# Eight more tokens a layer by gathered expert rows: 152 dense columns, a ring of twelve tiles, the picks turned at tile 60

## The reference, cut to what matters

```python
def peer_ffn(h, w_q, sub_keys, u_tab, v_tab):
    ...
        v_half, i_half = lax.top_k(sc, PEER_TOPK_HALF)
        ...
        top_s, pos = lax.top_k(cand, PEER_TOPK)
        expert = jnp.take_along_axis(cand_idx, pos, axis=-1)
        g = jax.nn.softmax(top_s, axis=-1)
        u = u_tab[expert]
        act = jax.nn.gelu(jnp.einsum('thkd,td->thk', u, xc).astype(jnp.float32), approximate=False)
        w = (g * act).astype(xc.dtype)
        return jnp.einsum('thk,thkd->td', w, v_tab[expert])
```

## Time and profile before

| | us |
|---|---|
| median of 3 runs | 1905.86 |
| lowest, highest | 1900.08, 1906.43 |
| profiled execution, device time | 1903.83 |
| its span, first to last instruction | 1902.1 |
| TensorE busy | 1857.0 |
| VectorE busy | 1354.1 |
| ScalarE busy | 484.7 |
| GpSimd busy | 442.0 |

### The profile page before, as it was taken

The page is one execution under the profiler, slowest core; times in us unless marked ns, Lnnn a source line. Parts: engine busy times, 40 slices in busy tenths (PEclk is TensorE's granted clock), DMA queues, the critical chain, the costliest instruction groups (busy, mean ns, idle before and its releaser), DMA issues. The chain is left out here.

```text
span 1902.1 us, 35435 instructions
## 1 busy us (share of the span) xinstructions
PE 1857.0 (98%) x13794; PEld 1768.2 (93%) x13794; DVE 1354.1 (71%) x2860; ACT 484.7 (25%) x898; POOL 442.0 (23%) x412
## 2 busy tenths in 40 slices
PE   8999999999999999999999999999999999999998
PEld 7888887878999899999999998899989999999998
DVE  6899886795799767677754347769996776776442
ACT  6557644565411100000000046552110000000001
POOL 0000000000046343333343200002454333334330
PEclk9999999999999999999999999999999999999999
DMA  6554325533979999999999953287999999999995
GB/s 249 215 205 181 122 83 169 175 100 124 341 246 407 409 408 409 406 405 401 401 401 410 383 188 122 86 295 273 336 409 408 409 404 396 408 399 396 409 410 200
DMA packets 148012, 580.26 MB, mean 305 GB/s; under 512 B 13596, under 2 KB 13724, under 8 KB 145216
## 3 DMA queue, kind: packets, MB, share of 16 engines
q1 hardware_dynamic: 91712, 376.37, 51.9%
q0 software_dynamic: 56192, 202.47, 27.4%
HBM read 576.62 MB, written 1.05 MB: 304 GB/s over the span
## 5 line engine op out<-in xcount | busy, mean ns | idle before, releaser
L2682 PE MATMUL bank<-e_hidden,wbuf 128*128 (+1 forms) x4096 | 566.9, 300 | 0.0
L2682 PEld LDWEIGHTS bank<-e_hidden,wbuf 128*128 128x128 f32 x4096 | 557.7, 190 | 0.0
L2631 PE MATMUL bank<-h_dense,wbuf 128*128 128x160 f32 x3712 | 520.8, 301 | 8.3 <-DMA wbuf<-in_peer_u 6.8
L2631 PEld LDWEIGHTS bank<-h_dense,wbuf 128*128 128x128 f32 x3712 | 506.2, 190 | 14.1 <-issue 7.7
L276 ACT ACTIVATE tile_hi<-wbuf 128x1024 fp32r<-128x1024 f32 (+2 forms) x117 | 121.9, 1047 | 376.6 <-PE bank L2682 286.7
L284 DVE TENSOR_TENSOR tile_lo<-wbuf,tile_hi 128x1024 fp32r<-128x1024 f32 (+2 forms) x117 | 140.1, 1210 | 87.5 <-ACT tile_hi L276 86.8
L2471 POOL DMA_INDIRECT e_gbuf<-in_peer_rows,e_row_at x128 | 131.7, 1029 | 300.3 <-PE bank L2631 219.4
L2471 POOL DMA_INDIRECT e_gbuf<-in_peer_v,e_row_at x128 | 142.1, 1111 | 236.7 <-PE bank L2682 157.1
L2771 ACT ACTIVATE e_hidden<-bank 128x320 f32<-128x320 f32 x128 | 55.9, 437 | 518.7 <-PE bank L2631 518.6
L2492 DVE SCALAR_TENSOR_TENSOR x_tok<-e_gbuf,e_acts,x_tok 128x1024 f32<-128x1024 f32 x128 | 164.0, 1281 | 32.2 <-DMA e_gbuf<-in_peer_v,e_row_at 24.9
L386 PE MATMUL bank<-a_parts,tile_hi 128*128 128x512 f32 x512 | 178.2, 392 | 0.0
(11 more groups left out here) (408 smaller groups left out, 2651.4 us busy)
## 6 DMA issues: line engine op xcount, KB each, us to landing
wbuf<-in_peer_v SPq DMA_DIRECT2D x128, 1024.0 KB, 9.8
wbuf<-in_peer_u SPq DMA_DIRECT2D x116, 1024.0 KB, 11.8
wbuf<-in_w_in SPq DMA_DIRECT2D x16, 2048.0 KB, 7.4
wbuf<-in_peer_q SPq DMA_DIRECT2D x32, 512.0 KB, 4.5
wbuf<-in_hyb_in SPq DMA_DIRECT2D x16, 512.0 KB, 3.8
e_gbuf<-in_peer_u SPq DMA_DIRECT2D x8, 1024.0 KB, 10.7
wbuf<-in_mla_uq SPq DMA_DIRECT2D x9, 512.0 KB, 3.4
wbuf<-in_mla_in SPq DMA_DIRECT2D x8, 528.0 KB, 5.3
```

Source lines behind the costliest of these rows:

```text
L2631: last = nc.tensor.matmul(bank[:, j // 2 % 2, j % 2 * S:j % 2 * S + DENSE], tile[:, k * P:(k + 1) * P], h_dense[:, k, :], start=(k == 0), ...
L2682: last = nc.tensor.matmul(turned_x(g, k)[:, 0:DENSE], deep[:, slot, k * P:(k + 1) * P], hidden[:, bass.ds(a, 1), 0:DENSE].rearrange("p a t ...
```

## The change

Eight more tokens (`RARES`) of the dense ones go by rows: 152 columns are left. Each shares the partitions of a block in sixteen parts of eight picks, so they take 8 gathers of U and 8 of V, at the end of each list: 208 gathers a layer, paced as before between tiles 8 and 240. Their row numbers, shares and copies of x come by 48 small DMAs (three for each group of eight partitions), which POOL issues ahead of gathers 56 to 71. They count in `moved`, and ScalarE's wait behind pair 38 is now for all of them (`ALL_MOVED`), as is the one ahead of the tile that overwrites their source. Their sum has a buffer of its own (`sum_rare`), set to zero by VectorE, and a third matmul for each k in the fold.

The ring has twelve tiles (`DEEP`), over all three weight buffers, and four tiles are loaded early, not sixteen. U then starts at another place of the ring, so V does too (`V_PAIR`). The next layer's weights are loaded at slightly other points, and VectorE's first three roundings for them wait until the V tiles in their place are used. The picks are turned behind tile 60, not 56. A group more of eight dense tokens is gone, 19 a half.

```diff
 GATHERED = 64
 FEWS = 32
-DENSE = S - GATHERED - FEWS
+RARES = 8
+DENSE = S - GATHERED - FEWS - RARES
 HIDDEN = DENSE
-EARLY_TILES = 16
+SLOTS = 4
+EARLY_TILES = 4
+DEEP = 3 * SLOTS
...
-            "deep": wbuf[:, 0:2, :].rearrange("p w (j c) -> p (w j) c", c=TILE),
+            "deep": wbuf[:, 0:3, :].rearrange("p w (j c) -> p (w j) c", c=TILE),
...
-    FEW = slice(DENSE - P, GATHERED)
+    FEW, RARE = slice(GATHERED - FEWS, GATHERED), slice(GATHERED - FEWS - RARES, GATHERED - FEWS)
     SHARED = PICKS // 2
     EARLY = 2 * GBUFS
-    DOTS = SHARED + FEWS
+    DOTS = SHARED + FEWS + RARES
     ITEMS = 2 * DOTS
     FEW_BLOCK = [(slice(FEWS * n, FEWS * n + FEWS), slice(FEWS * n, FEWS * n + FEWS)) for n in range(P // FEWS)]
+    RARE_BLOCK = [(slice(RARES * n, RARES * n + RARES), slice(RARES * n, RARES * n + RARES)) for n in range(P // RARES)]
     MOVED = DMA * len(FEW_BLOCK)
+    ALL_MOVED = 3 * MOVED + 3 * DMA * len(RARE_BLOCK)
...
-    early = ([gbuf[:, 2 * n:2 * n + 2, :] for n in range(GBUFS // 2)] + [whole_tiles(56), whole_tiles(24)]
-             + [g["wbuf"][:, 2, :].rearrange("p (j c) -> p j c", c=TILE)[:, 2 * n:2 * n + 2, 0:D] for n in range(2)])
+    early = [gbuf[:, 2 * n:2 * n + 2, :] for n in range(EARLY_TILES // 2)]
...
+    x_rare = sb(f"{tag}_x_rare", [P, D])
+    sum_rare = stage[:, 76 * S:80 * S]
...
-    LAST_ROUND = NKEYS - STEP
-    EARLY_ROUNDS = EARLY_TILES // STEP
+    PAIRS, STAGE_PAIRS = DEEP // 2, NKEYS // 2
+    FIRST_PAIRS = (NKEYS - EARLY_TILES) // 2
+    pair_loaded = [*ring_loaded, *g["deep_loaded"]]
...
+    def loads_before(p):
+
+        return (M_U - p + SLOTS - 1) // SLOTS if p < SLOTS else i * (FIRST_PAIRS + STAGE_PAIRS) // PAIRS
...
     def load_first(sp):
-        for p in range(SLOTS):
-            ring_slots = [s % SLOTS for s in (2 * p, 2 * p + 1)]
+        for p in range(PAIRS):
+            tiles = [last_before(s % SLOTS) for s in (2 * p, 2 * p + 1)]
+            if p < SLOTS:
+                sp.wait_ge(lo_done, last_before(p) + 1)
             if p < SLOTS // 2:
-                sp.wait_ge(lo_done, max(last_before(s) for s in ring_slots + [p]) + 1)
+                sp.wait_ge(lo_done, max(tiles) + 1)
             else:
-                sp.wait_ge(lo_done, last_before(p) + 1)
-                sp.wait_ge(used, max(last_before(s) for s in ring_slots) + 1)
-            if p == SLOTS // 2:
-                load_early(sp, 6)
-            elif p > SLOTS // 2:
-                load_early(sp, 7)
-            load_pair(sp, EARLY_TILES + 2 * p, p)
-        with sp.Fori(EARLY_ROUNDS + 1, ROUNDS) as r:
-            for p in range(SLOTS):
-                sp.wait_ge(used, STEP * r + M_U - STEP + 2 * p + 2)
-                load_pair(sp, STEP * r + 2 * p, p)
-
-    def load_values(sp, a, p):
-        sp.dma_start(deep[:, 2 * p:2 * p + 2, 0:D], V[bass.ds(a, 2), :, :].rearrange("a p c -> p a c")).then_inc(ring_loaded[p], DMA)
+                sp.wait_ge(used, max(tiles) + 1)
+            load_pair(sp, U, EARLY_TILES + 2 * p, p)
+        rounds = FIRST_PAIRS // PAIRS
+        with sp.Fori(1, rounds) as r:
+            for p in range(PAIRS):
+                sp.wait_ge(used, DEEP * r + M_U + EARLY_TILES - DEEP + 2 * p + 2)
+                load_pair(sp, U, DEEP * r + EARLY_TILES + 2 * p, p)
+        for p in range(FIRST_PAIRS - rounds * PAIRS):
+            a = EARLY_TILES + rounds * DEEP + 2 * p
+            sp.wait_ge(used, M_U + a - DEEP + 2)
+            load_pair(sp, U, a, p)
+
+    V_PAIR = FIRST_PAIRS % PAIRS
+    V_HEAD = PAIRS - V_PAIR
 
     def load_second(sp):
-        with sp.Fori(0, ROUNDS) as r:
-            for p in range(SLOTS):
-                sp.wait_ge(used, STEP * r + M_V - STEP + 2 * p + 2)
-                load_values(sp, STEP * r + 2 * p, p)
+        for n in range(V_HEAD):
+            sp.wait_ge(used, M_V + 2 * n - DEEP + 2)
+            load_pair(sp, V, 2 * n, V_PAIR + n)
+        with sp.Fori(0, (STAGE_PAIRS - V_HEAD) // PAIRS) as r:
+            for p in range(PAIRS):
+                sp.wait_ge(used, DEEP * r + M_V + 2 * V_HEAD - DEEP + 2 * p + 2)
+                load_pair(sp, V, DEEP * r + 2 * V_HEAD + 2 * p, p)
...
-            sp.wait_ge(used, M_V + LAST_ROUND + 2 * (m % SLOTS) + 1)
+            sp.wait_ge(used, M_V + NKEYS - DEEP + 2 * (m % SLOTS) + 2)
...
-            if j < STEP + 5:
+            if j < STEP + EARLY_TILES // 2:
                 load_early(sp, j - STEP)
-            if j == STEP + 5:
-                sp.wait_ge(rows_ready, 3)
-                sp.wait_ge(xn_turned, 4)
-                load_early(sp, 5)
...
+            if SHARES_AT <= n < SHARES_AT + len(RARE_BLOCK):
+                rows, picks = RARE_BLOCK[n - SHARES_AT]
+                pool.dma_start(share_rare[rows, :], pick[RARE, 1, 2, picks]).then_inc(moved, DMA)
+                pool.dma_start(row_rare[rows, :], row_of_few[RARE, picks]).then_inc(moved, DMA)
+                pool.dma_start(x_rare[rows, :], x_scaled[RARE, :]).then_inc(moved, DMA)
+            if n == DOTS - RARES:
+                pool.wait_ge(moved, ALL_MOVED)
             if n >= EARLY:
                 pool.wait_ge(used, M_U + pace(n))
-            if n < GBUFS:
+            if n < EARLY_TILES:
                 pool.wait_ge(used, M_U + n + 1)
...
+            elif DOTS - RARES <= n < DOTS:
+                table, rows = U_ROWS, row_rare[:, n - DOTS + RARES:n - DOTS + RARES + 1]
...
+        elif n >= DOTS - RARES:
+            dve.wait_ge(moved, ALL_MOVED)
+            vectors, dot = x_rare[:, :], dots_rare[:, n - DOTS + RARES:n - DOTS + RARES + 1]
...
-    TURN_AT, FOLD_AT = 56, NKEYS - 4
+    TURN_AT, FOLD_AT = 60, NKEYS - 4
...
+        def turn_picks():
+
+            pe.wait_ge(soft_step, 4 * NT)
+            pe.wait_ge(sc_kept[1], 7)
...
+        pe.wait_ge(early_loaded, DMA * EARLY_TILES // 2 * (i + 1))
         for j in range(EARLY_TILES):
...
+        looped = (TURN_AT - EARLY_TILES) // DEEP
+        with pe.Fori(0, looped) as r:
+            for j in range(DEEP):
+                experts(r, DEEP, EARLY_TILES, j)
+        first = EARLY_TILES + looped * DEEP
+        for j in range(HALF_KEYS - first):
+            if first + j == TURN_AT:
+                turn_picks()
+            experts(0, DEEP, first, j)
...
-                for t, start, size, at in ((1, P + GATHERED, GATHERED, 0), (0, DENSE, FEWS, GATHERED)):
-                    nc.tensor.matmul(turned_x(g, k)[:, start:start + size], x[:, t, k * P:(k + 1) * P],
+                for total, start, size, at in ((x[:, 1, :], P + GATHERED, GATHERED, 0), (x[:, 0, :], P + FEW.start, FEWS, GATHERED),
+                                               (sum_rare, DENSE, RARES, GATHERED + FEWS)):
+                    nc.tensor.matmul(turned_x(g, k)[:, start:start + size], total[:, k * P:(k + 1) * P],
...
             if f == JUNK_OVER:
-                act.wait_ge(gather_used, GATHER_0 + EARLY + 1)
+                act.wait_ge(moved, ALL_MOVED)
...
             if f == FEW_AT:
-                act.wait_ge(moved, 3 * MOVED)
+                act.wait_ge(moved, ALL_MOVED)
                 act.wait_ge(gather_used, GATHER_0 + EARLY + FEWS)
...
+        act.wait_ge(gather_used, GATHER_0 + DOTS)
+        nc.scalar.activation(dots_rare[:, :], dots_rare[:, :], ACT.Gelu).then_inc(exps_done, 1)
...
+                if taken == DOTS + SHARED + FEWS:
+                    shared(slice(0, RARES), share_rare, dots_rare, NT + 2 + len(ACTS), 5 + len(ACTS))
...
+        nc.vector.memset(sum_rare[:, :], 0.0).then_inc(picks_kept, 1)
...
+            dve.wait_ge(used, M_NEXT - SLOTS + j + 1)
             rest_tile(nc, dve, g, M_NEXT + j)
```

More of the change, by code:

```diff
@@ L96 @@
 CST, _n = {}, 0
-for _name, _width in (("ident", P), ("causal", SC), ("freq64", 32), ("freq32", 16), ("iota", NKEYS), ("fold", GATHERED + FEWS)):
+for _name, _width in (("ident", P), ("causal", SC), ("freq64", 32), ("freq32", 16), ("iota", NKEYS), ("fold", GATHERED + FEWS + RARES)):
     CST[_name] = _n
@@ L100 @@
 NCST = _n
-ARENA = 36768
+ARENA = 36760
 ROW_POST, ROW_FFN, ROW_FINAL = 0, 1, 3
@@ L239, in const @@
     a = CST[name]
-    width = {"ident": P, "causal": SC, "freq64": 32, "freq32": 16, "iota": NKEYS, "fold": GATHERED + FEWS}[name]
+    width = {"ident": P, "causal": SC, "freq64": 32, "freq32": 16, "iota": NKEYS, "fold": GATHERED + FEWS + RARES}[name]
     return g["cst"][0:rows, a:a + width]
@@ L2441, in gpsimd @@
         for rows, picks in FEW_BLOCK:
-            pool.dma_start(x_few[rows, :], x_scaled).then_inc(moved, DMA)
+            pool.dma_start(x_few[rows, :], x_scaled[FEW, :]).then_inc(moved, DMA)
         pool.wait_ge(moved, MOVED)
@@ L2649, in tensor @@
             all_rows(early[j // 2][:, j % 2, :], j)
-        with pe.Fori(0, (TURN_AT - EARLY_TILES) // STEP) as r:
-            for j in range(STEP):
-                experts(r, STEP, EARLY_TILES, j)
-        pe.wait_ge(soft_step, 4 * NT)
-        pe.wait_ge(sc_kept[1], 7)
-        for row in range(3):
-            for t in range(NT):
```

(24 more changed lines are left out.)

67 lines of the change are left out of this document (38 added, 29 removed).

## The result

| | before | after |
|---|---|---|
| median, us | 1904.0 (4 runs) | 1961.8 (4 runs) |
| lowest, highest | 1900.1, 1906.4 | 1960.0, 1963.6 |
| profiled execution: device time, span | 1903.8, 1902.1 | 1963.6, 1961.5 |
| layer 0's expert stage | 521.0 to 1112.5 | 517.4 to 1140.0 |
| layer 1's expert stage | 1300.9 to 1893.2 | 1328.8 to 1952.5 |

The ratio is 1.030, with an interval of 1.029 to 1.032. The forecast was 1915 us, its range 1894 to 1933: the change costs some 58 us, not 11. All of it lies in the two expert stages, each of which is 31 us longer; what lies between them took 188.4 us and takes 188.8.

What follows compares the result with a forecast made beforehand. TensorE was taken to set the time before with DMA close behind, and DMA after the change. Two layers at 5.0 us more each plus 1 us for next weights, on 1903.83, gave 1915 us; range 1894 to 1933.

Steps and rivals of the forecast that it cites:

- Spread transfers: 48 small issues ahead of gathers 56 to 71: TensorE stands some 13 us near tile 82, counted as nothing.
- Rival B: Wait for small transfers outlasts the ring, deciding from 13 us of standstill: 17 us a layer uncovered, 1949 us; chance 0.13.
- The ledger of DMA: Expert stage to tile 241: DMA moves 438.5 units of 512 KB in 561.4 us, setting the time.
- stock at tile 241: Units still out when tile 241 ends: 16.5, with about one tile loaded ahead and some 2.5 gathers out.
- The early stretch: Stage start, 515 to 575 us: ring refills from tile 6, DMA idles only about 5 us.
- The fold: Behind tile 241, near the stage's end: 48 matmuls for 32 at 109 ns, 5.2 us against 3.5.
- 152 columns: Dense U and V matmuls at 127.7 ns: 27.4 us less TensorE work a layer, unseen because DMA is late.
- Turn at 60: Turning the picks: TensorE waits up to 5 us at the turn or tile 64, counted as none.
- next weights: Step from layer 0 to the next part: three roundings wait for last V tiles, 0 to 2 us, 1 taken.
- Rival A: Expert stages: DMA gives more or has unseen slack, 1894 at 417 GB/s, 1842 if never holding TensorE; chance 0.17.
- Rival C: Early stretch used worse or better: 1933 with 10 us idle and four tiles ahead, or 1905; inside the forecast's 0.70.

Runs made afterwards that it cites:

- 3: Changed kernel without the eight tokens' gathers: 160 dense columns, 192 gathers, keeping the ring of twelve, four early tiles and turn at 60; 1893.0 us.
- 1: Changed kernel without the 48 small transfers a layer and the waits for them, rare gathers using other blocks' row numbers; 1937.9 us.
- 2: Changed kernel with the 16 copies of x issued before all gathers and ScalarE not waiting for later transfers; 1941.8 us.
- 6: Changed kernel with the fold's 48 matmuls in four parts of twelve, one ahead of each of the last four tiles; 1956.8 us.
- 4: Copies-of-x-first kernel (2) with dense matmuls of 128 columns for 152, extra gathers kept; 1932.7 us.
- 5: Kernel without the eight tokens' gathers (3), with dense matmuls of 128 columns for 160; 1881.0 us.
- tenth experiment: Kernel with copies of x first and the fold in parts (seventh), each pair of V tiles issued six tiles later; 1938.2 us.
- seventh: Changed kernel with both the copies of x issued first and the fold in four parts; 1934.4 us.

## Why the forecast was wrong

**The account by parts.** The medians differ by 11.0 us less for the ring (3), 44.9 more for eight tokens by 16 gathers a layer at 152 columns (1 less 3), 3.9 for the spread issues (2 less 1) and 20.0 for ScalarE's wait and the copies (changed kernel less 2). Such differences add up to 1961.8 whatever they mean. The traces take them apart, at the start of the fold; both stages together, in us:

| | before | ring alone (3) | no small transfers (1) | copies first (2) | changed |
|---|---|---|---|---|---|
| up to the fold | 1158.9 | 1151.7 | 1186.9 | 1188.6 | 1212.1 |
| fold and last four tiles | 24.9 | 24.9 | 35.9 | 29.3 | 34.2 |

Up to the fold the gathers cost 35.2, the spread issues 1.7, and the wait with the copies 23.5. The folds would take 27.6 in the last three kernels without a fall of the clock (13.8 each, as in 6); what lies above that, 8.3, 1.7 and 6.6 us, hides in the differences of the medians.

**The account by the forecast's own steps**, for layer 0, measured from the start of the stage (its first U tile). Tile 241's end is read three tiles of 2.04 us ahead of the gap that stands before the last eight tiles and the fold (after: 1106.28 - 0.68 - 6.1 = 1099.5).

| | before | forecast | no small transfers | after |
|---|---|---|---|---|
| tile 241 ends, us after the start | 555.4 | 560.4 | 570.1 | 582.1 |
| blocks moved up to there | 420.8 | 438.5 | 443.9 | 443.1 |
| DMA idle up to there, us | 22.8 | 5 | 7.9 | 20.9 |
| from there to the end of the stage, us | 36.1 | 35.8 | 42.2 | 40.5 |

The blocks come from windows that begin 6 us ahead of the stage, as the forecast's did; 395 GB/s over 588.08 us are 443.1 of 512 KB, and at 1.280 us each 567.2 us. These are before, after, and the kernel without small transfers:

```profile
514.97:1076.40 561.43, 556.48 (x4552) 551.75 (x4553) 400.93 (x872) 41.09 (x83) 217.29 (x200) 1.00 1.00 393
```

```profile
511.42:1099.50 588.08, 543.00 (x4521) 533.28 (x4522) 413.80 (x864) 40.21 (x84) 286.46 (x264) 0.97 1.01 395
```

```profile
509.15:1085.20 576.05, 545.09 (x4521) 532.12 (x4522) 414.94 (x864) 40.29 (x84) 264.59 (x216) 0.99 1.02 404
```

- **Spread transfers, the step that failed most.** They were counted at nothing, because "about ten ring tiles are empty by then and take 12.8 us to load". TensorE stood 14.05 us, and DMA lost about as much, 12.0 us a layer by the table (582.1 less 570.1). Not ten tiles of the ring were empty but four: TensorE had already stood 4.9 and 5.9 us for one-hots, at 662.8 and 685.3, and the ring filled meanwhile. Of these waits the forecast had only the first, as its up to 5 us at tile 64. They are not the small transfers' work for the most part: the first ends ahead of gather 56, and without those transfers they are 3.6 and 5.5 us (1). There DMA stays at 409 GB/s all the same, since the gathers go on every 2.4 us. Here they came at POOL's pace, taken as 2.8 us a gather and measured as 3.7: ten of the sixteen gather issues took 1.5 to 1.9 us for 0.94, and POOL stood some 6 us more. So DMA ran at 347 GB/s from 680 to 700 us, before the long hole began, and had little but gathers to move in it. Rival B's mechanism is what happened, but its point of decision, 13 us of standstill, was set too late: with four tiles to load it is 5.1 us. The forecast had 13 us a layer as this term's own bound, which makes 1941, and left it out of a range that ends at 1933. VectorE waited 24.2 us for gathers between 660 and 730, and 17.7 in the same stretch of the first experiment. VectorE's wait (us in total, times, longest):

```profile
DVE e_gbuf L2508 <- DMA e_gbuf<-in_peer_rows,e_row_at: 24.2, 16, 4.4
```

- **The ledger of DMA, right in kind.** DMA does set the time now (4, 5), and 16 more gathers with their copies cost, up to the fold of the two kernels of 128 columns, (1182.2 - 1140.5 - 1.7) / 2 = 20.0 us a layer for 21.8 computed; the medians give 23.9, of which 5.0 lie in the fold and the last tiles. Its mis-sized term is the stock at tile 241: 16.5 blocks were to be out, with one tile loaded ahead; some 11 were, in every kernel with full loads. That is 5 blocks, 6.5 us a layer. A V pair took 22.1 us from issue to landing, of which 2.56 are its own 1 MB at 409.5 GB/s; so several pairs are under way at once (five at 1099.5, by the issues and landings in the trace) when TensorE waits for the oldest, and the 5 blocks are what is already there of them. The tenth experiment, with half the ring, took this from 444.0 blocks (the seventh) to 440.9, which supports the reading; that it would gain time did not come true, since the idle time rose from 9.3 to 17.9 us. The issues of V pairs between 700 and 1090 us (count, KB, median us from issue to landing), after and then in the tenth experiment:

```profile
wbuf<-in_peer_v SPq DMA_DIRECT2D x60, 1024.0 KB, 22.1
```

```profile
wbuf<-in_peer_v SPq DMA_DIRECT2D x58, 1024.0 KB, 9.6
```

- **The early stretch.** 5 us idle were taken, 7.9 measured up to tile 241 without the small transfers; 360 to 373 GB/s from 515 to 575 us in the kernels with twelve tiles and four early ones, for 278 before. Nearly right, 3 us short.
- **The fold.** 5.2 us were taken for 48 matmuls and 8.2 for the last four tiles, 13.4; they took 17.1, since the granted clock fell (0.81 and 0.85 in the windows above). This, a gap of 0.7 us at tile 244 and 0.3 for the matmuls' 129.8 ns make the 4.7 us between 40.5 and 35.8. In the first experiment the same takes 18.8 us in layer 0.
- **152 columns.** 127.7 ns were taken; 128 matmuls start over 1122.89 - 1106.28 = 16.61 us, 129.8 ns. As forecast, the saving is hardly seen in the time.
- **Turn at 60** and **next weights**: 2.7 us of wait at the turn in layer 0 and 4.9 at tile 64, 7.6 for at most 5; DMA ran at 409 GB/s from 640 to 660 us meanwhile, so to count nothing was right. 0.4 us between the layers for 1.
- **Rival A** falls: no slice of the page passes 410 GB/s within a stage. **Rival C**'s mechanism, four tiles ahead at tile 241, was the ledger's miss, priced inside the range. Without the holes the time is still 1937.9 us, 5 above the range, and 8 of it are the clock's fall in that run's folds: the ledger and the fold together pass the range, and the holes add 24 to that.

Per layer the terms are 12.0 for the small transfers, 6 for the stock, 3 for the early stretch and 5 for the fold, 26 on a stage forecast at 596; it took 622.6. Layer 0's stage began 3.6 us sooner, at 517.4, which the forecast had left as it was; the sixth experiment, the same kernel up to the fold, began it at 520.4, so this is no more than the spread between executions.

## What to carry to other kernels

Where an engine's wait is to be hidden by a ring, count how full the ring will be at that moment, after the smaller waits that come first; an empty ring covers a hole, a full one passes it on to DMA. A step that moves issues onto a queue slows everything that is paced by that queue: follow it to the engine that takes those results in order, and to what it owes to others. And where DMA sets the time, a block that is fetched instead of computed costs its bytes in full: 16 blocks and the copies cost some 20 us a layer, and the matmul columns that they replaced saved next to nothing (24 columns less save 3 us a layer up to the fold, experiment 4).

## What the runs showed of the hardware

The granted clock, 1.00 before in all of these stretches, fell in two places. Behind holes: a mean of 0.66 from 720 to 740 us, so partly at the lower of its two levels, 1.2 GHz, after TensorE had stood for 14.05 us; the sixteen matmuls behind that wait took 4.42 us, where sixteen at 129.8 ns take 2.1. The Trainium skill (TensorE: Matmul & The Clock Gate, section "HAM oscillation — how this bites in real kernels") tells of such a fall in the waits for DMA between matmuls; the trace shows it in a wait for ScalarE.

The other place is the fold, where TensorE did not stand at all: 48 matmuls of 64, 32 or 8 columns in a row, and four of them, which took 0.53 to 0.61 us at first, took 1.04 towards the end. The 32 of the kernel before, 64 or 32 columns wide, showed no fall; neither did twelve at a time between tiles (6, 7, 10). In the second experiment the fall came late in layer 0 and not at all in layer 1 with the same 48 matmuls, so what decides it is not settled.

The pairs of V tiles landed 10.0 us after their issue before, at 404 GB/s from 700 to 1090 us, 23.0 in the seventh experiment at 409, and 9.6 in the tenth at 401: with more of the ring in flight each pair took twice as long, and at most 2% more was moved. U's pairs in the same stretch show no such growth (12.3 us before, 11.3 in the seventh). The Trainium skill (DMA: Bandwidth & Descriptors, section "SWDGE vs HWDGE vs iDMA") says that each DMA engine takes the queues of the software and the hardware way in turn. That fits a gather that takes a share of the rate from the pair that TensorE waits for; no run here shows the turns themselves.
